# Turning key pages two at a time in a MoBA + gMLP decode step on one Trainium2 core

## The reference

```python
PAST_LEN, PAGE_SIZE, N_HEADS, HEAD_DIM, MOBA_BLOCK, MOBA_TOPK = 2048, 128, 8, 64, 256, 3

q, k, v, g_a, u, v_n, g_b, m_a, m_b = mixer_inputs(x, ...)      # one projection of rmsnorm(x)
attn = moba_prompt(...) ; attn_s = moba_sample(q, k, v, cache_k, cache_v, page_table, rel_bias)
...
def moba_sample(...):            # for each of 8 batches: 16 pages of 128 keys, 8 blocks of two pages
    k_full = cache_k[layer, page_table[:, :n_full * ppb]]
    k_mean = mean over the 256 keys of a block
    gate   = einsum('bthd,bnhd->bhtn', q, k_mean)
    sel    = top_k(gate, 3)                                     # three blocks per row and head
    p      = softmax([q . k_sel + bias, q . k_own + bias])
    out    = p . [v_sel, v_own]
...
x + W_o( sig(m_a) * P_a(attn * silu(g_a)) + sig(m_b) * P_b(sgu * silu(g_b)) ), then a final rmsnorm
```

## Time and profile before

| what | value |
| --- | --- |
| median of 3 runs | 621.86 us (620.78 to 622.79) |
| the profiled execution's own time | 621.19 us |
| its span, first to last instruction | 618.9 us |
| PE busy | 576.7 us (93%) |
| DVE busy | 314.6 us (51%) |
| ACT busy | 215.2 us (35%) |
| mean granted TensorE clock | 0.988 of full speed |
| DMA moved | 112.50 MB, mean 182 GB/s |

### The profile page before, as it was taken

How to read it: one execution, slowest core, us unless ns; L and a number is a source line. 1 busy time by engine, 2 the same in 40 slices (tenths; PEclk the granted TensorE clock), 3 DMA queues, 4 the chain that set the end, 5 groups by cost and what they waited for, 6 DMA issues and landing times.

```text
span 618.9 us, 15227 instructions
## 1 busy us (share of the span) xinstructions
PE 576.7 (93%) x6242; PEld 540.6 (87%) x6242; DVE 314.6 (51%) x695; ACT 215.2 (35%) x466; POOL 33.1 (5%) x42
## 2 busy tenths in 40 slices
PE   3899998999999999999999989999999999979990
PEld 2799998999899899999889978989999989979990
DVE  5532223436446555655855745873642455952306
ACT  5422322332433434444544442232443231323213
POOL 1310120100000000000000000020000001100002
PEclk9999999999999999999999999999999999989996
DMA  8337332564775866767658578786798572332003
GB/s 296 115 106 253 104 117 93 190 173 126 228 227 183 242 202 191 219 207 226 203 173 254 173 231 256 240 257 181 218 341 298 169 245 70 121 127 69 1 1 144
DMA packets 73990, 112.50 MB, mean 182 GB/s; under 512 B 5417, under 2 KB 38194, under 8 KB 73922
## 3 DMA queue, kind: packets, MB, share of 16 engines
q1 hardware_dynamic: 72690, 108.18, 55.1%
q0 software_dynamic: 1232, 3.36, 1.7%
HBM read 106.98 MB, written 4.53 MB: 180 GB/s over the span
## 4 chain that ended last, share of the span: by engine, by line
PE 75%; DVE 15%; ACT 5%; issue 3%; DMA 2%; SPq 0%; POOL 0%; DVEq 0%; ACTq 0%; POOLq 0%
PE BK L455 46%; PE BK L575 7%; PE BK L587 4%; PE BK L601 4%; PE BK L475 3%; PE BK L651 2%; DVE WL L997 2%; DVE G L1278 1%; PE BK L668 1%; PE BK L658 1%; ACT WH L799 1%; DVE XR L1018 1%; ACT SC L897 1%; ACT FJ L976 1%; DMA SGC<-in_gating_constants 1%
## 5 line engine op out<-in xcount | busy, mean ns | idle before, releaser
L455 PE MATMUL BK<-XH,WH 128*128 128x272 f32 x704 | 223.7, 318 | 1.4 <-DVE XL L1027 1.4
L455 PE MATMUL BK<-XH,WL 128*128 128x272 f32 x704 | 204.1, 290 | 0.0
L455 PE MATMUL BK<-XL,WH 128*128 128x272 f32 x704 | 203.0, 288 | 0.0
L455 PEld LDWEIGHTS BK<-XH,WH 128*128 128x128 f32 x704 | 133.2, 189 | 12.2 <-issue 9.2
L455 PEld LDWEIGHTS BK<-XL,WH 128*128 128x128 f32 x704 | 133.8, 190 | 0.5 <-issue 0.5
L455 PEld LDWEIGHTS BK<-XH,WL 128*128 128x128 f32 x704 | 133.1, 189 | 0.0
L997 DVE TENSOR_TENSOR WL<-WRAW,WH 128x1024 fp32r<-128x1024 f32 x56 | 68.6, 1224 | 100.7 <-ACT WH L799 100.6
L575 PE MATMUL BK<-CST,KRAW 128*128 128x128 f32 x512 | 77.1, 273 | 2.4 <-DVE ATS L1171 2.2
L1091 DVE COPY KT<-BK 128x512 f32<-128x512 f32 x64 | 44.2, 691 | 57.1 <-PE BK L575 57.0
L799 ACT ACTIVATE WH<-WRAW 128x1024 fp32r<-128x1024 f32 x60 | 63.2, 1053 | 18.0 <-PE BK L475 18.0
L575 PEld LDWEIGHTS BK<-CST,KRAW 128*128 128x128 f32 x512 | 60.2, 140 | 4.4 <-issue 4.1
(11 more groups left out here) (186 smaller groups left out, 776.6 us busy)
## 6 DMA issues: line engine op xcount, KB each, us to landing
KRAW<-in_cache_k SPq DMA_DIRECT2D x128, 256.0 KB, 3.5
VRAW<-in_cache_v SPq DMA_DIRECT2D x120, 256.0 KB, 3.7
WRAW<-in_w_in SPq DMA_DIRECT2D x22, 1024.0 KB, 5.7
WRAW<-in_w_o SPq DMA_DIRECT2D x4, 1024.0 KB, 5.1
XR<-in_x_prompt SPq DMA_DIRECT2D x4, 512.0 KB, 6.4
VEX<-in_cache_v SPq DMA_DIRECT2D x8, 256.0 KB, 4.6
WRAW<-in_w_pb SPq DMA_DIRECT2D x4, 512.0 KB, 6.8
WRAW<-in_w_pa SPq DMA_DIRECT2D x4, 512.0 KB, 5.2
```

The lines of the kernel that those rows point to most:

```text
L455: last = mm(BK[h][:, 0:HALF], w[:, n % 2, k, :], x[:, k, cols], start=(k == 0 and w is WH and x is XA), stop=(k == KC - 1 and w is WL))
```

## The change

PE turns pages `t` and `t + 1` one after the other in each even step, before that step's filling, and none in odd steps. DVE evicts page `t + 1` in the even step. The places in the lists are the same as before; only the parity changes. What depended on the old order is moved with it: the wait on the local part (`lm_ev`) stands at the page with `i % 16 == 7` instead of 5, borrowing the odd bank in an even step (`turn_local`) now waits for the page turned in that same step, and `sample_out` stands in DVE's list at `t % 16 == 5` instead of 6.

```diff
@@ turn_page (PE)
                     wait(pe, kt_dve, i // 2)
-                    if i >= 21 and i % 16 == 5:
+                    if i >= 23 and i % 16 == 7:
                         pe.wait_ge(lm_ev, i // 16)
@@ other_bank (PE)
                     pe.wait_ge(kt_act, min(t // 2 + 1, 64))
                 else:
-                    pe.wait_ge(kt_dve, min(t // 2, 64))
+                    pe.wait_ge(kt_dve, min(t // 2 + 1, 64))
@@ the steps (PE)
             for t in range(STEPS):
-                if t < PAGES:
+                if t % 2 == 0 and t < PAGES:
                     turn_page(t)
+                    turn_page(t + 1)
                 run(fill, 2)
@@ the steps (DVE)
-                if t % 2 == 1 and t < PAGES:
-                    page_out(t)
+                if t % 2 == 0 and t < PAGES:
+                    page_out(t + 1)
                 if t % 4 == 2 and 22 <= t < 86:
                     prompt_gate(t // 4 - 5)
-                if t % 16 == 6 and t >= 38:
+                if t % 16 == 5 and t >= 37:
                     sample_out(t // 16 - 2)
```

## The result

The changed kernel takes 629.86 us (median of 4 runs, 627.88 to 632.18) against 622.33 for the kernel before in the same comparison: a ratio of 1.0114, with a 95% interval of 1.0083 to 1.0146. It is slower by 1.1%; the forecast was 628.4 us and 1.0%. Its profiled execution took 628.02 us with a span of 625.9, 7.0 us more than the span before.

A forecast was written before the change was run, and what follows sets the result against it. PE, busy 93% of the span, was taken as the bound. Pairing -0.3 and terms +3.5, +3.7, +0.3, -0.5 sum to +6.7 us, rounded to 6.5 on 621.9: 628.4 us, 1.0% slower; range 621.5 to 631.5, chance 0.60.

The forecast's parts named there:

- Turning in pairs: On PE, the second page of a pair costs what a page alone costs; -0.3 us taken over 64 pairs.
- The rival that pairing saves changes between kinds of matmuls: On PE, half the changes of operand kind go, making the kernel faster; 618.8 us at 0.15 per pair; chance 0.12.
- Term 1: At t % 4 == 2, prompt_gate stands behind the key copy, so PE's prompt scores wait 0.30 us, 12 times: +3.5 us.
- Term 2: At t % 16 == 0, the key copy delays block sums and later prompt scores delay the chain: +3.7 us over five batches.
- Term 3: turn_local, in the bank of this step's page, waits for DVE's copy behind WL in step 100: +0.3 us.
- Term 4: sample_out a step earlier removes two page-turn waits, but the SGC load takes back the step 86 gain: -0.5 us.
- Absorbed: Rival: later chain waits take up the new prompt waits, leaving some +1, 622.9 us, no measurable change; chance 0.17.
- Key loads late: Rival: even pages' loads are needed four steps later instead of five; ten late by half a microsecond give 633 us; chance 0.11.

The follow-up runs named there:

- both moves: Changed kernel with DVE's copy of page t + 1 moved behind prompt_gate and, in t % 16 == 0 steps, behind block sums and APT copy: 623.30 us, ratio 1.0011.
- the gate first: Changed kernel with prompt_gate moved in front of the copy of page t + 1 in DVE's list, at t % 4 == 2: 624.97 us, ratio 1.0042.
- experiment 2: Changed kernel with DVE's copy of page t + 1 behind the block sums and APT copy, only at t % 16 == 0 (16 to 112): 629.63 us, ratio 1.0102.
- experiment 5: Kernel with both moves, PE turning page t + 1 behind prompt_scores in the 16 steps that have them, DVE copying it behind prompt_max: 622.48 us, ratio 1.0002.
- experiments 6: Kernel before, nothing paired, with sample_out at t % 16 == 5 instead of 6 in DVE's list: 621.81 us, ratio 0.9971.
- experiment 7: Kernel before, unpaired, with sample_out at t % 16 == 5 and step 84's mixing loads issued before the value loads: 619.50 us, ratio 0.9935.
- the copy in the odd step: Changed kernel, PE still pairing, but DVE evicts the odd page in the odd step except where t % 16 == 4: 625.03 us, ratio 1.0031.
- experiment 9: Changed kernel with both moves in DVE's list and the mixing loads in front of the value loads: 620.22 us, ratio 0.9953.

## Why the prediction was right, step by step

**Turning in pairs.** Eight transposes last 1.03 us, as forecast, and the filling starts 0.79 after the first. The second page costs what a page alone costs. The forecast took -0.3 for all pairs. With both moves the shift at the prompt scores goes from 0.56 in step 18 to 0.46 in step 78, so 30 pairs gave 0.1 at most, and the early `sample_out` alone gives as much (-0.08 to -0.22 over the same steps). No gain of pairing is shown. The rival that pairing saves changes between kinds of matmuls needed 0.10 us per pair, 6.4 us in all; it is excluded.

**Term 1.** Forecast 0.30 us at 12 places, which is 3.6; the working writes +3.5. In step 22 the scores start 2.07 after the first transpose, forecast 2.02, and 1.72 with the gate first, so 0.35. Over the loop the size can be read from the starts of the prompt scores, as they lie behind the kernel before: 1.01, 1.33, 1.67 and 2.00 us in steps 18 to 30, then 2.99, 3.22, 3.52, 3.80, then 4.79, 5.01, 5.35, 5.66, then 6.31, 6.48, 6.77, 7.07. The twelve steps of term 1 add 3.4 together. PE's list has 3.8 us in 15 places, three of them the batch steps, and 2.8 for the twelve, less than the shifts give. Putting the gate first took 4.96 us off, forecast 4.3 at most, because it takes the gate's part of the batch steps too, most of all in step 66 (0.65 to 0.06). The rule of the Trainium skill that was weighed (VectorE: DVE Perf Modes, The DRAIN you can't avoid), read as time behind the instruction, would have had the gate start 1.11 after the copy's start; it starts 0.61 after it (166.39 to 167.00), as in the earlier trace rows. That section of the Trainium skill also says that a next instruction which is not held starts earlier; the working left that out, and the measured 0.61 is earlier than the 0.69 that the copy lasts.

**Term 2.** Forecast +3.7 over five batches. The same row of shifts gives it batch by batch: 0.57 at step 16 (1.01 less the 0.44 of the page that is turned earlier), 0.99 by step 34, 0.99 by step 50, 0.65 by step 66, and 0.49 at the turn of step 83 (7.12 less 7.07 - 0.44), 3.7 together. Forecast were 0.6, 1.0, 1.0, 0.6 and 0.45. I worked it out at the prompt values; in the trace the same delay shows first at the gate sums (six waits, 3.2) and only its rest at the values (four, 0.9), which was in the working (the 0.61) but not in my list of what to look for. Both parts are confirmed: the copy in front of the block sums (experiment 2, 1.34 where 1.8 was expected, and 1.69 once the gate was out of the way), and the later prompt scores (experiment 5, 0.45 at step 80, as forecast; the other 0.5 there is not this chain).

**Term 3.** One wait of 0.2 us at step 100, forecast 0.3. The list has no other.

**Term 4.** Both waits on `sample_out` are gone and `turn_mixing` waits 2.5 us for SGC, forecast about 2. That the first of the two gains would be eaten by the load was argued from one row; experiments 6 and 7 show it, the one by moving `sample_out` alone, the other by taking the load out of the way. The size was off by 0.3: the two waits gave 2.2 and the load took 2.0 (0.5 to 2.5), so -0.2 where -0.5 was forecast. With term 3 that makes nothing, and between steps 83 and 131 the changed kernel neither loses nor gains against the one before (7.12 and 7.11).

**The sum.** The profiled execution was forecast at 627.9 us and took 628.02; the loop grew by 7.1 where the terms add to 6.7. That the whole came within 0.1 us is partly luck, since the parts outside the loop scatter by more. The median lies 1.5 us over the forecast: two of the four runs are at 631.69 and 632.18. Those executions have no trace here, only a mean granted clock: 0.981 for the one at 632.18, against 0.988 for the two near 628. Over 626 us that is 4.4 us lost (an estimate: 0.007 x 626), and it is 4.2 us longer, so a low clock would account for it. The one at 631.69 has 0.987, which by the same reckoning is 0.6 us; what made it longer is open.

**The rivals.** *Absorbed*: no later wait took up the gate's; the turn of the probabilities took up 0.5 us only (3.3 to 2.8). *Key loads late*: no wait on a load of KRAW is in the list, although such a load now lands in 3.7 us instead of 3.5 at the median and in 8.9 at most. The tightest window of four steps held; how much was to spare was not measured.

## What to carry to other kernels

Where engines run hand-written lists in order, moving an instruction costs what stands behind it: of a change "two at once in every other step" price the producer's side (here nothing), then for each thing that now stands behind the bigger piece ask who waits for it. A piece moved to the head of a list should start from inputs that are ready; DVE's copy was put in front of an instruction that had been ready for a step, and took its 0.3 us twelve times. And a wait that is removed is only worth what the next wait leaves: take away the load behind it first (here `sample_out` alone gave 0.6, and 3.4 with the load's issue moved as well).

## What the runs showed of the hardware that was not expected

**The clock behind a short idle time.** In the kernel with the gate first, PE idles 2.26 us for the SGC load, the granted clock stays at 1.00 through the idle time and falls behind it. Windows of two microseconds; after the five engines' busy times come the granted clock, the DMA's share and its GB/s:

```profile
372.00:374.00 2.00, 0.83 (x7) 0.60 (x5) 0.00 (x0) 0.00 (x0) 0.00 (x0) 1.00 1.07 292
374.00:376.00 2.00, 0.91 (x6) 0.91 (x7) 0.00 (x0) 0.00 (x0) 0.00 (x0) 0.89 1.03 320
376.00:378.00 2.00, 2.00 (x11) 2.00 (x10) 0.00 (x0) 0.00 (x0) 0.00 (x0) 0.50 0.72 278
378.00:380.00 2.00, 2.00 (x15) 1.95 (x13) 0.99 (x2) 1.83 (x3) 0.00 (x0) 0.76 0.02 8
```

0.50 is the lower of the two levels, 1.2 GHz; filling matmuls then start 0.225 apart instead of 0.125, and the pair of pages lasts 1.59 us instead of 1.03:

```profile
376.70 0.43 PE L455 MATMUL BK<-XL,WH 128*128 128x272 f32 x1
376.92 0.43 PE L455 MATMUL BK<-XH,WL 128*128 128x272 f32 x1
...
377.83 1.59 PE L575 MATMUL BK<-CST,KRAW 128*128 128x128 f32 x8
```

Against the kernel before, this execution loses 1.4 us between steps 83 and 131, where the changed kernel loses nothing. The same happened in the profiles with the copy last and with the copy in the odd step (waits of 2.78 and 2.57 us). It did not happen in the profile with `sample_out` early, with a wait of 2.58, nor in the changed kernel's own, with one of 2.46:

```profile
378.00:380.00 2.00, 0.00 (x0) 0.00 (x0) 0.00 (x0) 0.00 (x0) 0.00 (x0) 1.00 1.09 236
380.00:382.00 2.00, 1.79 (x15) 1.79 (x16) 0.00 (x0) 0.00 (x0) 0.00 (x0) 1.00 1.03 356
```

So a wait of PE of some 2.5 us can cost 4: the idle time, and in some executions 1.5 more behind it. The length of the wait alone doesn't decide it, as the pair of 2.57 and 2.58 shows. Nor was it the only place. In the profile of experiment 7 the clock falls ahead of the loop, behind PE's wait of 1.7 us for LMX near 100 us, which every kernel here has; it does so in the profile of experiment 9 too, and in none of the other nine:

```profile
104.00:106.00 2.00, 2.00 (x12) 2.00 (x11) 0.00 (x0) 0.00 (x0) 0.00 (x0) 0.51 0.43 155
```

Its profiled span (619.3) is 0.4 us longer than that of the kernel before, although its loop is 3.4 us shorter and its median is lower. The loop begins 3.6 us later, and the clock near 104 us is the smaller part of that.

**A slower start that the granted clock does not show.** The profile with `sample_out` early has a granted clock of 1.00 all the way to its loop, which still begins 2.2 us later than before (113.77 against 111.53). The delay arises between 24 and 30 us: filling matmuls start 0.225 apart there up to 29.4 us, as they do at the lower clock, where in the kernel before they start 0.125 apart from 24.8 on. First `sample_out` early, then the kernel before:

```profile
25.40 0.43 PE L455 MATMUL BK<-XH,WL 128*128 128x272 f32 x1
25.63 0.43 PE L455 MATMUL BK<-XH,WH 128*128 128x272 f32 x1
```

```profile
24.93 0.29 PE L455 MATMUL BK<-XH,WL 128*128 128x272 f32 x1
25.06 0.29 PE L455 MATMUL BK<-XH,WH 128*128 128x272 f32 x1
```

For the first of these stretches the window gives the granted clock as 1.00 all the same:

```profile
24.00:26.00 2.00, 1.91 (x10) 1.71 (x10) 1.57 (x4) 0.28 (x1) 0.00 (x0) 1.00 0.86 245
```

The profile of experiment 7 has the same slow stretch, up to 28.9 us, and the fall near 104 us on top. So at least two things, a fall of the granted clock behind a wait and a longer slow stretch at the start, cost an execution some 1.5 and 2.2 us where they occur. The kernel before spreads over some 5 us (620.56 to 625.66 over all comparisons), and its mean granted clock explains only part of that: its runs at 0.989 lie between 620.56 and 624.5. How much of the rest is the start was not measured, since only one execution of each kernel has a trace.
